# Two chunks of keys in one product: the intra-chunk levels of the recurrences in a two-layer hybrid decoder step

## The chip, the cores and the metric

The kernel runs on one core of one Trainium2 chip (trn2). The metric is the time of one execution in microseconds (us), taken on the device. The kernel before ran three times, at 1866.79 to 1868.54 us with a median of 1867.7 us. A fourth execution was recorded by the hardware profiler; its rows are the ones shown here.

The engines go by short names: PE is TensorE's matmul, PEld its load of the stationary operand, DVE is VectorE, ACT is ScalarE, POOL is GpSimd, SP is SyncE, which only starts DMAs.

## The reference, cut to what matters

The program is two decoder layers over 512 prompt positions and 64 positions of eight short sequences (eight positions each). In each layer a token mixer has three groups of heads. Six heads are windowed attention. The other ten, four HGRN2 heads with 64 keys' features and six GLA heads with 32, are gated linear recurrences, which the reference computes in chunks of 64 positions:

```python
def step(S, blk):
    qc, kc, vc, gc = blk
    b = jnp.cumsum(gc, axis=1)
    o_inter = jnp.einsum('bthk,bhkv->bthv', qc * jnp.exp(b), S)
    diff = b[:, :, None] - b[:, None, :]
    decay = jnp.exp(jnp.where(causal, diff, -jnp.inf))
    A = jnp.einsum('bthk,bshk,btshk->bths', qc, kc, decay)
    o_intra = jnp.einsum('bths,bshv->bthv', A, vc)
```

The change is about `A`, the 64 x 64 matrix of each head and chunk. Its decay depends on the pair of positions and on the feature, so it is no plain product of queries and keys. After the mixer come the output projection, an MLP of width 4096 with squared ReLU and a gated per-layer embedding.

## The kernel before, in words

All tensors are feature-major: features on the 128 partitions, the 576 positions along the row. Weights come in units of 128 x 1024 numbers. Each is split by ACT and DVE into a leading and a remaining part, and each product with weights is three `fp32r` products (lines 738 to 742 in the mixer, 1684 to 1686 in the MLP) that move 288 positions past a stationary 128 x 128 block.

`A` is built by levels. `LEVELS` is 0, 1, 2, 4, 8, 16, 32. Level 0 is the diagonal. At a level of size h each chunk is cut into blocks of 2h positions; every pair (key in the earlier half of a block, query in the later half) belongs to this level, and there the decay falls apart into a factor for the key and one for the query, both measured from the block's middle. DVE takes the differences (`diff`, lines 1443 and 1444), ACT exponentiates them (`decays`, line 1200), and DVE multiplies the earlier halves with the keys and the later halves with the queries (`scale`, lines 1450 and 1452). So `LV[l % 2]`, the tile that the level's products read, holds keys in the earlier half of each block and queries in the later.

The products of a level run by `GROUPS`: four groups of two heads and two of one. For each head, PE multiplies keys and queries of each of the eight chunks, 64 keys stationary and 64 queries moving (line 887), and writes chunk c to the upper or lower 64 partitions of a PSUM bank by c's parity. The tile is used as keys and as queries at once, so only a part of each 64 x 64 result means anything. The groups take turns on two banks; a group waits until DVE has emptied the one before the last (`lv_ev`). DVE's `pick` copies the entries that the level's mask names into `AT` with one predicated copy a group (line 1470, 512 or 256 numbers in each of 128 partitions). In the levels that fit in eight positions (sizes 0 to 4, `SMALL`) line 898 adds one 64 x 64 product a head for the short sequences, and line 1478 its copy.

The order around the levels is written out by hand. In levels 0 to 5 PE does 18 products of one projection between groups 1 and 2 and the other 30 after group 5 (`project`). In levels 4 to 6 it also does the partners of the rotary embedding (line 861) ahead of groups 2 and 4, which ACT copies (line 1234) and DVE's `rotate` uses (lines 1457 to 1460). PE enters a level when DVE has scaled it (`lv_ready`). After level 6 PE multiplies `AT` by the values (lines 916 and 924), and the attention begins. SP starts the first keys' loads after the last `lv_ready`, the others after the last projection.

All products of the levels are full fp32: each shows in the trace as two records of LDWEIGHTS and MATMUL.

Of the kernel before, what the change touches and what calls it, by code (L numbers as in the profile page):

```python
# [16 lines left out]
P = 128  # L17
# [211 lines left out]
def build(nc, x_t, consts, params, w_first, p_t, s0_in, w_units, ck, cv,  # L229
          y_out, kp_out, kn_out, vp_out, vn_out, ck_out, cv_out, sp_out, ss_out):  # L230
    with ExitStack() as ctx:
# [183 lines left out]
        for layer in range(DEPTH):  # L415
# [233 lines left out]
            def _(pe):  # L649
# [216 lines left out]
                for l in range(len(LEVELS)):  # L866
# [7 lines left out]
                    for g, heads in enumerate(GROUPS):  # L874
# [6 lines left out]
                            pe.wait_ge(*at(lv_ev, gi - 1))  # L881
                        for i, h in enumerate(heads):
                            r, row, n = HEAD_AT[h]
                            for c in range(NC):
                                o = 64 * (c % 2)
                                col = (4 * i + c // 2) * CH
                                mm = nc.tensor.matmul(b_[o:o + 64, col:col + CH],  # L887
                                                      kq[0][row:row + n, r, c * CH:(c + 1) * CH],
                                                      kq[1][row:row + n, r, c * CH:(c + 1) * CH], start=True, stop=True)
                        mm.then_inc(*up(lv_mm, 1))  # L890
                        gi += 1
                        if l in SMALL:
# [441 lines left out]
            def _(dve):  # L1334
# [129 lines left out]
                def pick(l):  # L1464
                    nonlocal gi, si
                    mask = con[:, C_MASK + CH * l:C_MASK + CH * (l + 1)].bitcast(U32).rearrange("p (a t) -> p a t", a=1)
                    for g, heads in enumerate(GROUPS):
                        n, s = len(heads), FIRST_SLOT[g]
                        dve.wait_ge(*at(lv_mm, gi + 1))
                        nc.vector.copy_predicated(  # L1470
                            AT[:, s:s + n].rearrange("p s c t -> p (s c) t"), mask.to_broadcast([P, 4 * n, CH]),
                            bank[4 + gi % 2][:, 0:4 * n * CH].rearrange("p (a t) -> p a t", t=CH)).then_inc(*up(lv_ev, 1))
                        gi += 1
                        if l >= 4 and g == 1:
                            rotate(2 * l - 8)
                        if l in SMALL:
                            dve.wait_ge(*at(ls_mm, si + 1))
                            nc.vector.copy_predicated(
                                ATS[0:NEW, s:s + n], mask[0:NEW].to_broadcast([NEW, n, CH]),
                                bank[6 + si % 2][0:NEW, 0:n * CH].rearrange("p (a t) -> p a t", t=CH)).then_inc(*up(ls_ev, 1))  # L1480
                            si += 1
# [829 lines left out]
```

## Time and profile before

| | us |
|---|---|
| median of three runs | 1867.7 |
| the profiled execution's own time | 1867.47 |
| its span, first to last instruction | 1865.7 |
| PE busy / PEld busy in the span | 1769.5 / 1646.6 |
| DVE busy / ACT busy | 858.2 / 653.0 |
| line 887, PE busy, both layers | 75.4 |
| line 1470, DVE busy, both layers | 52.6 |

The last number is the sum of two groups, 40.5 us for the copies of 512 numbers and 12.1 us for those of 256. "Busy" is time covered by at least one record. Matmuls overlap in their pipeline and the ends of their records are modelled, so the distance from one record's start to the next says more about PE than a record's duration does; where equal instructions are merged into one row, x32 with 1.15 us means that 32 of them covered 1.15 us. Levels 0 to 6 run from 186.9 to 278.1 us in the first layer and from 1107.7 to 1206.4 us in the second.

### The profile page before, as it was taken

To read this page: it belongs to the slowest core of one execution; us is meant where nothing else is said; L and a number is where in the kernel's file an instruction comes from. 1 tells how busy PE (TensorE), PEld (TensorE's weight loads), DVE (VectorE), ACT (ScalarE), POOL (GpSimd) and SP (SyncE) were. 2 spreads that over 40 slices of the span, in tenths; PEclk is the share of its full clock that TensorE was granted. 3 is DMA by queue.
4 is the path that set the end of the run, shared out by engine and by line. 5 is a ranking of instruction groups with operands and counts; after the bars stand their busy time and mean duration, and the time that the engine had idled before them with its cause. 6 is when DMAs were issued, how large, how long until landed. Compare 5 with 4: busy or idle time off the path is not lost.

```text
span 1865.7 us, 35758 instructions
## 1 busy us (share of the span) xinstructions
PE 1769.5 (95%) x16070; PEld 1646.6 (88%) x16070; DVE 858.2 (46%) x1311; ACT 653.0 (35%) x963; POOL 71.1 (4%) x90
## 2 busy tenths in 40 slices
PE   6999998899999999999889999987999999999998
PEld 5988985588999999998888888845989999999988
DVE  5514885336423333346544157844354133333365
ACT  5422425544423222233344232245344231222233
POOL 0012110000000000000000130100000000000000
PEclk9999998899999999999989998988999999999999
DMA  7521428851836625442353132388419366355311
GB/s 265 179 68 60 160 82 338 306 179 69 310 125 216 217 101 205 158 137 68 111 206 110 58 132 77 123 336 297 155 64 317 123 214 217 110 193 181 123 58 63
DMA packets 60649, 303.67 MB, mean 163 GB/s; under 512 B 7120, under 2 KB 8784, under 8 KB 58832
## 3 DMA queue, kind: packets, MB, share of 16 engines
q1 hardware_dynamic: 53072, 200.91, 30.1%
q0 software_dynamic: 7424, 100.47, 15.4%
q8 instruction: 127, 2.08, 0.5%
q14 instruction: 26, 0.21, 0.0%
HBM read 290.74 MB, written 111.08 MB: 215 GB/s over the span
## 4 chain that ended last, share of the span: by engine, by line
PE 88%; DVE 7%; ACT 3%; issue 2%; DMA 1%; SPq 0%; DVEq 0%; ACTq 0%
PE pair L1684 15%; PE pair L1686 14%; PE pair L1685 14%; PE pair L887 3%; PE pair L738 3%; PE pair L740 2%; PE pair L742 2%; PE pair L720 2%; PE pair L670 2%; PE pair L721 2%; PE pair L722 2%; PE pair L671 2%; PE pair L672 2%; PE pair L1764 2%; PE pair L996 1%
## 5 line engine op out<-in xcount | busy, mean ns | idle before, releaser
L1684 PE MATMUL pair<-x_hi_part,w_hi_part 128*128 128x288 f32 x1088 | 322.2, 296 | 2.0 <-DVE tmp L2063 2.0
L1685 PE MATMUL pair<-x_lo_part,w_hi_part 128*128 128x288 f32 x1088 | 321.0, 295 | 0.0
L1686 PE MATMUL pair<-x_hi_part,w_lo_part 128*128 128x288 f32 x1088 | 319.9, 294 | 0.0
L2000 DVE TENSOR_TENSOR w_lo_part<-raw,w_hi_part 128x1024 fp32r<-128x1024 f32 x154 | 188.7, 1225 | 234.8 <-ACT w_hi_part L1851 234.8
L1684 PE MATMUL pair<-u_hi_part,w_hi_part 128*128 128x288 f32 x928 | 274.7, 296 | 0.0
L1685 PE MATMUL pair<-u_lo_part,w_hi_part 128*128 128x288 f32 x928 | 273.8, 295 | 0.0
L1686 PE MATMUL pair<-u_hi_part,w_lo_part 128*128 128x288 f32 x928 | 272.8, 294 | 0.0
L1851 ACT ACTIVATE w_hi_part<-raw 128x1024 fp32r<-128x1024 f32 x154 | 161.8, 1051 | 209.6 <-PE pair L1686 208.3
L1684 PEld LDWEIGHTS pair<-x_hi_part,w_hi_part 128*128 128x128 f32 x1088 | 203.9, 187 | 2.5 <-DVE tmp L2063 2.5
L1686 PEld LDWEIGHTS pair<-x_hi_part,w_lo_part 128*128 128x128 f32 x1088 | 204.9, 188 | 0.0
L1685 PEld LDWEIGHTS pair<-x_lo_part,w_hi_part 128*128 128x128 f32 x1088 | 204.3, 188 | 0.0
L1686 PEld LDWEIGHTS pair<-u_hi_part,w_lo_part 128*128 128x128 f32 x928 | 174.8, 188 | 0.0
L1685 PEld LDWEIGHTS pair<-u_lo_part,w_hi_part 128*128 128x128 f32 x928 | 174.2, 188 | 0.0
L1684 PEld LDWEIGHTS pair<-u_hi_part,w_hi_part 128*128 128x128 f32 x928 | 173.9, 187 | 0.0
L1340 DVE TENSOR_TENSOR win_part<-raw,win_part 128x1024 fp32r<-128x1024 f32 x54 | 65.9, 1224 | 175.0 <-ACT win_part L1103 174.9
L1915 ACT ACTIVATE tmp<-tmp 128x576 f32<-128x576 f32 x64 | 44.0, 687 | 255.6 <-DVE tmp L2063 255.6
L738 PE MATMUL pair<-xn_hi_part,win_part 128*128 128x288 f32 x352 | 114.6, 326 | 0.0
L2063 DVE SCALAR_TENSOR_TENSOR tmp<-pair,tmp 128x576 f32<-128x576 f32 x64 | 48.5, 757 | 135.6 <-PE pair L1686 122.1
L740 PE MATMUL pair<-xn_lo_part,win_part 128*128 128x288 f32 x352 | 109.8, 312 | 0.0
L742 PE MATMUL pair<-xn_hi_part,win_part 128*128 128x288 f32 x352 | 109.6, 311 | 0.0
L2072 DVE TENSOR_TENSOR y<-y,pair 128x576 f32<-128x576 f32 x42 | 31.7, 755 | 157.6 <-PE pair L1686 157.6
L670 PE MATMUL pair<-xn_hi_part,win_part 128*128 128x288 f32 x256 | 79.0, 308 | 10.2 <-DVE xn_lo_part L1340 9.9
(282 smaller groups left out, 3552.3 us busy)
## 6 DMA issues: line engine op xcount, KB each, us to landing
raw<-w_units SPq DMA_DIRECT2D x210, 512.0 KB, 3.6
ck_out<-ck POOLq DMA_DIRECT2D x16, 3060.0 KB, 14.0
arena<-cv SPq DMA_DIRECT2D x24, 640.0 KB, 7.8
tail<-cv SPq DMA_DIRECT2D x24, 640.0 KB, 7.9
arena<-ck SPq DMA_DIRECT2D x18, 640.0 KB, 10.1
more<-ck SPq DMA_DIRECT2D x18, 640.0 KB, 12.9
h<-ck SPq DMA_DIRECT2D x12, 640.0 KB, 12.7
y_out<-h SPq DMA_DIRECT2D x16, 288.0 KB, 2.1
```

The source lines that it names most:

```text
L670: nc.tensor.matmul(out, wh[:, cols], XH[:, k, t], start=k == 0, stop=False)
L738: mm = nc.tensor.matmul(out, wh[:, cols], XH[:, k, t], start=k == 0, stop=False)
L740: mm = nc.tensor.matmul(out, wh[:, cols], XL[:, k, t], start=False, stop=False)
L742: mm = nc.tensor.matmul(out, wl[:, cols], XH[:, k, t], start=False, stop=k == KT - 1)
L887: mm = nc.tensor.matmul(b_[o:o + 64, col:col + CH], kq[0][row:row + n, r, c * CH:(c + 1) * CH], kq[1][row:row + n, r, c * CH:(c + 1) * CH] ...
L1340: return tt_(dst, src, hi.bitcast(F32), ALU.subtract).then_inc(*up(done, 1))
L1684: nc.tensor.matmul(out, wh[:, cols], xh[:, k, t], start=n == 0, stop=False)
L1685: nc.tensor.matmul(out, wh[:, cols], xl[:, k, t], start=False, stop=False)
L1686: mm = nc.tensor.matmul(out, wl[:, cols], xh[:, k, t], start=False, stop=n == KT - 1)
L1851: return A(dst, src, ACT.Copy).then_inc(*up(done, 1))
L2000: return tt_(dst, src, hi.bitcast(F32), ALU.subtract).then_inc(*up(done, 1))
L2063: stt(two(t), home(f"up{g}")[:, :, 0:HALF], 0.0, two(RS), ALU.max, ALU.mult).then_inc(*up(lin_ev, 1))
```

## The change

In levels 1 to 6 a product takes the 128 positions of two neighbouring chunks as the stationary operand, and moves 64 queries: of both chunks only the later halves of the blocks, picked by a strided view. The result covers 128 partitions (the keys of both chunks) by 64 columns (32 late queries of the first chunk, then 32 of the second). What meets across the two chunks is not used. Four products a head and level stand where eight did, 40 a level for the ten heads. Level 0 keeps its form.

DVE's copy is split by the parity of the chunk: one takes partitions 0 to 63 with the columns of the even chunks, the other partitions 64 to 127 with those of the odd ones. Each handles half as many numbers in a partition, in 64 partitions, and writes to and masks by strided views. Two instructions a group stand where one did; the second signals.

```diff
-                            for c in range(NC):
-                                o = 64 * (c % 2)
-                                col = (4 * i + c // 2) * CH
-                                mm = nc.tensor.matmul(b_[o:o + 64, col:col + CH],
-                                                      kq[0][row:row + n, r, c * CH:(c + 1) * CH],
-                                                      kq[1][row:row + n, r, c * CH:(c + 1) * CH], start=True, stop=True)
+                            if l == 0:
...
+                            else:
+
+                                for c2 in range(TT):
+                                    t, col = slice(2 * c2 * CH, 2 * (c2 + 1) * CH), (4 * i + c2) * CH
+                                    late = kq[1][row:row + n, r, t].rearrange("p (b a e) -> p b a e", a=2, e=LEVELS[l])[:, :, 1]
+                                    mm = nc.tensor.matmul(b_[:, col:col + CH].rearrange("p (b e) -> p b e", e=LEVELS[l]),
+                                                          kq[0][row:row + n, r, t], late, start=True, stop=True)
...
+                            e = LEVELS[l]
+                            late = mask.rearrange("p z (b a e) -> p z b a e", a=2, e=e)[:, :, :, 1]
+                            for par_ in range(2):
+                                rows = slice(64 * par_, 64 * par_ + 64)
+                                dst = AT[rows, s:s + n].rearrange("p s c (b a e) -> p (s c) b a e", a=2, e=e)[:, :, :, 1]
+                                src = bank[4 + gi % 2][rows, 0:4 * n * CH].rearrange("p (x z b e) -> p x z b e", z=2, e=e, b=CH // 2 // e)
+                                ins = nc.vector.copy_predicated(dst, late[rows].to_broadcast([64, 4 * n, CH // 2 // e, e]), src[:, :, par_])
+                            ins.then_inc(*up(lv_ev, 1))
```

On PE, the first two groups of level 1 in the first layer, between two projections. The shape is that of the output, partitions by columns; line 896 is the new product and line 906 the old line 898.

```order
 L742 MATMUL pair<-xn_hi_part_104,win_part_106 128x288
-L887 MATMUL pair<-arena 64x64 x16
-L898 MATMUL pair<-arena 64x64 x2
-L887 MATMUL pair<-arena 64x64 x16
-L898 MATMUL pair<-arena 64x64 x2
+L896 MATMUL pair<-arena 128x64 x8
+L906 MATMUL pair<-arena 64x64 x2
+L896 MATMUL pair<-arena 128x64 x8
+L906 MATMUL pair<-arena 64x64 x2
 L738 MATMUL pair<-xn_hi_part_104,win_part_107 128x288
```

Nothing changes place: the groups, the products for the short sequences and the projections follow each other as before, with half as many products of 128 output partitions in a group. Every neighbour of a line-906 product inside these groups now has another output shape.

On DVE, the end of the picks of level 1 in the first layer, first of the kernel before.

```order
L1470 COPY_PREDICATED tail<-con,pair 128x512
L1478 COPY_PREDICATED tail<-con,pair 64x128
L1470 COPY_PREDICATED tail<-con,pair 128x256
L1478 COPY_PREDICATED tail<-con,pair 64x64
L1450 TENSOR_TENSOR arena<-arena 128x576x2
```

The same place in the changed kernel, where 1490 is the line of the split copy and 1458 that of the first multiplication.

```order
L1490 COPY_PREDICATED tail<-con,pair 64x256 x2
L1497 COPY_PREDICATED tail<-con,pair 64x128
L1490 COPY_PREDICATED tail<-con,pair 64x128 x2
L1497 COPY_PREDICATED tail<-con,pair 64x64
L1458 TENSOR_TENSOR arena<-arena 128x576x2
```

Two copies of half the length stand where one stood, and the rest keeps its order.

## Rows read from the trace of the kernel before

**Rows 1.** The page: busy time of each engine, and the chain that ended last.
```profile
PE 1769.5 (95%) x16070; PEld 1646.6 (88%) x16070; DVE 858.2 (46%) x1311; ACT 653.0 (35%) x963; POOL 71.1 (4%) x90
...
PE 88%; DVE 7%; ACT 3%; issue 2%; DMA 1%; SPq 0%; DVEq 0%; ACTq 0%
```

**Rows 2.** Stretches of both layers' levels: PE, PEld, DVE, ACT, POOL busy, clock, DMA.
```profile
186.90:278.10 91.20, 88.03 (x1515) 81.50 (x1514) 75.73 (x109) 29.93 (x28) 12.20 (x15) 0.96 0.32 115
...
1110.00:1207.00 97.00, 92.27 (x1460) 85.59 (x1463) 75.70 (x110) 27.63 (x26) 12.24 (x15) 0.89 0.30 109
```

**Rows 3.** PE, line 887's groups by form: count, busy us, mean ns, idle before.
```profile
L887 PE MATMUL pair<-arena 32*64 32x64 f32 x1344 | 46.2, 223 | 3.1 <-DVE tail L1470 3.1
...
L887 PE MATMUL pair<-arena 64*64 64x64 f32 x896 | 29.2, 224 | 3.7 <-DVE arena L1452 3.7
```

**Rows 4.** Timeline of level 6, first layer, PE alone: start us, us covered, line, idle before.
```profile
269.54 1.91 PE L887 MATMUL pair<-arena 64*64 64x64 f32 x64
271.38 1.24 PE L861 MATMUL pair<-tail,con 128*128 128x288 f32 x4
...
276.26 1.29 PE L887 MATMUL pair<-arena 32*64 32x64 f32 x32 [0.63 <-DVE tail L1470]
```

**Rows 5.** Timeline, level 0 begins: start us, us covered, engine, line, count, idle before.
```profile
186.67 0.29 PE L742 MATMUL pair<-xn_hi_part,win_part 128*128 128x288 f32 x1
186.89 1.15 PE L887 MATMUL pair<-arena 64*64 64x64 f32 x32
...
188.86 0.39 PE L898 MATMUL pair<-arena 64*64 64x64 f32 x4
...
189.19 0.40 PE L738 MATMUL pair<-xn_hi_part,win_part 128*128 128x288 f32 x1
```

**Rows 6.** Timeline in narrow windows: line 861, first and third of three records.
```profile
271.73 0.41 PE L861 MATMUL pair<-tail,con 128*128 128x288 f32 x1
...
272.21 0.41 PE L861 MATMUL pair<-tail,con 128*128 128x288 f32 x1
```

**Rows 7.** Durations of one line's records (min/median/max ns): 32, 64, 128 stationary columns.
```profile
L988 PEld LDWEIGHTS pair<-tail,arena x96: 106/110/110, 285.8 to 1275.3; 128*32 128x32 f32 x96
...
L887 PEld LDWEIGHTS pair<-arena x32: 129/135/135, 186.9 to 187.8; 64*64 64x64 f32 x32
L887 PE MATMUL pair<-arena x30: 218/218/267, 186.9 to 187.8; 64*64 64x64 f32 x30
...
L861 PEld LDWEIGHTS pair<-tail,con x4: 186/190/190, 271.4 to 272.0; 128*128 128x128 f32 x4
L861 PE MATMUL pair<-tail,con x4: 406/406/510, 271.4 to 272.2; 128*128 128x288 f32 x4
```

**Rows 8.** Timeline at 186.89 us, narrow windows: loads of line 887 come in pairs.
```profile
186.89 0.14 PEld L887 LDWEIGHTS pair<-arena 64*64 64x64 f32 x2 [0.17 <-issue]
...
186.89 0.19 PEld L887 LDWEIGHTS pair<-arena 64*64 64x64 f32 x4 [0.17 <-issue]
```

**Rows 9.** Timeline: 32 records that move 8 columns past 64 stationary, and what follows.
```profile
165.70 1.10 PE L795 MATMUL pair<-tail 64*64 64x8 f32 x32
166.63 0.89 PEld L802 LDWEIGHTS pair<-tail 64*64 64x64 f32 x27
```

**Rows 10.** Timeline, narrow windows: attention scores, two row halves, 128 stationary columns each.
```profile
312.72 0.19 PEld L948 LDWEIGHTS pair<-tail 64*128 64x128 f32 x2 [0.17 <-issue]
...
312.83 0.19 PEld L948 LDWEIGHTS pair<-tail 64*128 64x128 f32 x2
```

**Rows 11.** Timeline near 132 us: first and third of three records of a projection.
```profile
132.10 0.29 PE L738 MATMUL pair<-xn_hi_part,win_part 128*128 128x288 f32 x1
...
132.36 0.30 PE L742 MATMUL pair<-xn_hi_part,win_part 128*128 128x288 f32 x1
```

**Rows 12.** DVE, groups by form: count, busy us, mean ns, idle before.
```profile
L1470 DVE COPY_PREDICATED tail<-con,pair 128x512 f32<-128x512 uint32 x56 | 40.5, 740 | 14.7 <-PE pair L887 14.1
...
L1470 DVE COPY_PREDICATED tail<-con,pair 128x256 f32<-128x256 uint32 x28 | 12.1, 441 | 5.4 <-PE pair L887 5.2
L1478 DVE COPY_PREDICATED tail<-con,pair 64x128 f32<-64x128 uint32 x32 | 9.0, 282 | 0.0
```

More of the change, by code:

```diff
@@ L883, in _ @@
                             r, row, n = HEAD_AT[h]
-                            for c in range(NC):
-                                o = 64 * (c % 2)
-                                col = (4 * i + c // 2) * CH
-                                mm = nc.tensor.matmul(b_[o:o + 64, col:col + CH],
-                                                      kq[0][row:row + n, r, c * CH:(c + 1) * CH],
-                                                      kq[1][row:row + n, r, c * CH:(c + 1) * CH], start=True, stop=True)
+                            if l == 0:
+                                for c in range(NC):
+                                    o = 64 * (c % 2)
+                                    col = (4 * i + c // 2) * CH
+                                    mm = nc.tensor.matmul(b_[o:o + 64, col:col + CH],
+                                                          kq[0][row:row + n, r, c * CH:(c + 1) * CH],
+                                                          kq[1][row:row + n, r, c * CH:(c + 1) * CH], start=True, stop=True)
+                            else:
[4 more added lines that the diff above has]
+                                                          kq[0][row:row + n, r, t], late, start=True, stop=True)
                         mm.then_inc(*up(lv_mm, 1))
@@ L1469, in pick @@
                         dve.wait_ge(*at(lv_mm, gi + 1))
-                        nc.vector.copy_predicated(
-                            AT[:, s:s + n].rearrange("p s c t -> p (s c) t"), mask.to_broadcast([P, 4 * n, CH]),
-                            bank[4 + gi % 2][:, 0:4 * n * CH].rearrange("p (a t) -> p a t", t=CH)).then_inc(*up(lv_ev, 1))
+                        if l == 0:
+                            nc.vector.copy_predicated(
+                                AT[:, s:s + n].rearrange("p s c t -> p (s c) t"), mask.to_broadcast([P, 4 * n, CH]),
+                                bank[4 + gi % 2][:, 0:4 * n * CH].rearrange("p (a t) -> p a t", t=CH)).then_inc(*up(lv_ev, 1))
+                        else:
+                            e = LEVELS[l]
[6 more added lines that the diff above has]
+                            ins.then_inc(*up(lv_ev, 1))
                         gi += 1
```

## The prediction

> **What bounds the kernel now.** I read the page first. The reader is to see PE busy for 95% of the span, and a chain that ended last of which 88% is PE [rows 1]. What lengthens PE in a stretch without idle time lengthens the kernel. Then I cut out the levels: in the first layer PE is busy for 88.0 of 91.2 us, in the second for 92.3 of 97.0, while DVE is busy for 75.7 in each [rows 2]. So here too PE sets the end, and DVE has 15 us or more of room a layer. Then the waits of line 887: 3.1 us in both layers for DVE's copies and 3.7 us for its scaling [rows 3]. A gain on DVE could give back at most these 6.8 us. The question is what a product of the new form costs PE.
>
> **What a product costs PE.** Each full fp32 product is two records, each with its own load of the stationary operand. I take distances between starts. In level 6 two groups, 64 records, run from 269.54 to the start of line 861 at 271.38 [rows 4]: 1.84 us, 29 ns each, and 27 when 0.09 are taken off for the change of shape behind them (below). In level 0, 32 records cover 1.15 us; less the 0.22 of the last one that is 0.93 us over 31 distances, 30 ns [rows 5], with a slower first one in it. I take 28 ns: a level of 160 records is 4.5 us, with bounds of 4.4 (27 ns) and 4.9 (30.6 ns, 0.98 us a group).
>
> Which part binds, stream or load? Line 861 moves 288 columns past a 128-column operand with (272.21 - 271.73) / 2 = 0.24 us between starts [rows 6], 0.83 ns a column, so 64 columns stream in 53 ns. The loads: medians are 110, 135 and 190 ns for 32, 64 and 128 stationary columns [rows 7], about 0.83 ns more for each column, over a constant of some 83. The constant is latency, the rest is occupation: 27, 53 and 107 ns. A second row says the same. The first record of a run has nothing to hide its load behind, and is longer than its successors by 510 - 406 = 104 ns with 128 columns and by 267 - 218 = 49 ns with 64 [rows 7].
>
> How, then, can line 887 start a record every 28 ns? Its loads come in pairs: two are done within the first 0.14 us, four within 0.19 [rows 8], one pair every 50 to 60 ns. Neighbouring chunks go to the lower and the upper 64 columns of the array, and each half works for itself: 53 to 60 ns a record in a half, two halves at once. That this is the load and not the stream is shown by line 795, which moves only 8 columns and still needs 166.63 - 165.70 = 0.93 us for 32 records, 29 ns each, 58 in a half [rows 9].
>
> The new product takes all 128 columns. There is no second half to run beside it, its heads share their rows within a group, and one load lasts 107 ns and covers the 53 ns of the stream. Line 948 is the nearest row with 64 x 128 operands: its two first loads go at once to two different row halves, and each half's next one comes 0.11 us later [rows 10]. So the distance is 107 ns: half as many records, each nearly four times as far apart, 80 x 0.107 = 8.6 us a level instead of 4.5, +4.1. For six levels in two layers: **+49.2 us**. Bounds: from 4.9 us before, 8.56 - 4.90 = 3.66, or +43.9; and at the 131 ns (132.36 - 132.10 over two [rows 11]) of the projections' chain, which has a load of the same width behind a stream of 288 columns, 10.5 - 4.4 = 6.1, or +73. That chain is fp32r, with a longer stream, so the loads' own rows are nearer and I stay with them.
>
> The Trainium skill, "TensorE: Matmul & The Clock Gate", section "LDWEIGHTS (loading the stationary operand)", gives columns divided by 1.2 as the load's nanoseconds, 107 for 128 and 53 for 64. By this rule the sum is the same; what speaks against the change is only its consequence, that the column count and not the number of instructions is paid. The same page's tiling part says that a load overlaps running matmuls only when the row group differs. By that rule the sum would be another: see the third rival.
>
> **Changes of shape.** Before, lines 887 and 898 follow each other in one shape. Now the products for the short sequences (64 output partitions) stand between products of 128. Such a change is seen at 186.67: the first load of line 887 comes 0.22 us after line 742's start, where the distance in the chain is 0.13 [rows 11], and then waits 0.05 for its load, 0.14 in all. On the way back line 738 comes 0.16 us after the last start of line 898 (188.86 + 0.17 = 189.03), where 0.06 were usual: 0.10 [rows 5]. Mean 0.12. In levels 1 to 3 there are 3 such changes in the first block and 7 in the second, 10 a level, 60 in both layers: **+7.2 us**. Bounds 0 and 0.20 each, 0 to 12 us. The Trainium skill, "TensorEngine Tiling (Array Packing)", section "Key Properties", says that changing the tiling mode drains TensorE. The trace agrees, with 0.22 against 0.13.
>
> **DVE.** The copy of 512 takes 740 ns and that of 256 takes 441, 1.17 ns a number over some 140; 128 numbers then take 290, and the row of a 128-number copy says 282 [rows 12]. A double group costs 2 x 441 instead of 740, +0.14; a single one 2 x 282 instead of 441, +0.12. Per level 4 x 0.14 + 2 x 0.12 = +0.8, per layer +4.9. No row shows copies with such strides. Between no penalty and half the rate (1.17 ns more a number: 256 x 1.17 = 0.30 for each of eight copies and 0.15 for each of four, +3.0 a level), I take none, since the operands' strides are small. Either way it lies beside PE: DVE's 75.7 us become 81 or, at worst, 99, while the stretch becomes 118. Only the very last copies of level 6 are on the path, at +0.1 us. **0 us**. If PE were not slower, this cover would be gone: the fourth rival.
>
> **Waits given back.** Line 887's 3.1 us of waiting for copies [rows 3] come from groups that PE finishes faster than DVE empties the bank (0.9 us and 0.45 against 0.74 and 0.44). Now a group takes 1.7 or 0.86 us and DVE is in time; 0.63 of it is in level 6 [rows 4], where DVE rotates in between. Level 0's part stays. **-2.5 us**. The 3.7 us for the scaling [rows 3] stay: the products of level 0 ahead of them aren't changed. What is late next is nothing; PE runs through. **Low clock:** of the new time a few per cent fall where the granted clock is 1.2 GHz (mean 0.96 and 0.89 [rows 2]) and count double: 5 to 10% of it in the second layer would be +2; most such places are at the entry of level 1, so **+1 us**. SP and POOL issue what they did, later with everything else.
>
> Sum: 49.2 + 7.2 + 0 - 2.5 + 1 = +54.9 us. The profiled execution took 1867.47 us, 1.8 outside its span and 0.2 below the median, so 1867.5 + 54.9 = 1922.4, and **1922 us**.
>
> **The rivals.**
> 1. Loads wait in one queue, at 28 ns for 64 columns and 56 for 128. The even distance of lines 887 and 795 allows this reading. Then 80 x 0.056 = 4.5, no change on PE; shape changes +7.2 and waits -2.5 remain: 1872. Against it: two loads within 0.14 us [rows 8], and the first record's 104 ns.
> 2. Faster. The full-width load uses the paths of both halves, 53 ns, so that only the stream of 53 ns binds: 80 x 0.053 = 4.24, -0.26 a level, -3.1 in twelve; the waits go too, -2.5, and if shape changes within the same rows cost nothing, 1862. It decides as soon as the distance between records falls under 56 ns. For it: half the loads and half the instructions. Against it the same 104 ns: line 861 is a full-width load, and its first record shows what it takes.
> 3. Load and stream of one tile don't overlap (the page's rule above, as a mechanism here): 107 + 53 + 5 = 165 ns, 80 x 0.165 = 13.2, +8.7 a level, +104 in all, and +5.7 as above: about 1977. Against it line 861's 0.24 us, which is the stream alone, with a load of 104 ns hidden in the same rows [rows 6].
> 4. DVE takes the end, if 1 or 2 holds for PE and strided copies run at half rate: DVE needs 75.7 + 4.9 + 18 = 99 us a layer in a stretch of 91 to 97, +5 to +8 a layer and more where it is late already: about 1885.
> 5. The clock. PE streams less in a microsecond now. If the granted clock falls to 1.2 GHz for a sixth of the work of the levels, 2 x 118 / 6 = 39 us of it take twice as long: 1922 + 39, about 1960. For it: the second layer's levels already run at a mean of 0.89 [rows 2]. Against it: the first layer's, with the same products, run at 0.96, and no row shows the clock falling inside an unbroken run of them.
>
> **How the numbers follow.** A measurement of this kernel tells 0.2%, 3.7 us, from no change. The forecast gets 0.78, rival 1 0.07, rival 2 0.06, rival 3 0.03, rival 4 0.01, rival 5 0.05. Rival 1's 1872 lies at the edge; I give 0.04 of it to no change. So faster 0.06, same 0.04, slower 0.90. The forecast's own range is 1867.5 + 43.9 - 2.5 = 1909 to, with both upper bounds at once, 1867.5 + 73 + 12 + 1 - 2.5 = 1951; I cut the top at 1945, since the two rarely meet. I lower the low end to 1900, for waits given back that I don't see, and leave the rivals out, some 0.2 in all.
>
> **What would show it.** The new line has 80 records a level, some 107 ns apart, a double group in 1.7 us, its loads 186 to 190 ns long. Line 906 in levels 1 to 3 has gaps of 0.1 to 0.2 us around it. Levels 0 to 6 take about 118 us in the first layer instead of 91. PE no longer waits for the copies in levels 1 to 5. The split copies take 0.44 and 0.28 us. Distances of 55 to 61 ns would refute the step on the load, copies of 0.7 us the one on DVE, and low clock within the levels would make rival 5 real.

## The result and the profile after

The changed kernel takes 1962.1 us (median of 4 runs, 1955.1 to 1975.0) against 1868.1 us before on the same chip: a ratio of 1.053, 95% interval 1.050 to 1.056, or +94 us. The forecast was 1922 us with a range of 1900 to 1945. The direction was right and the size was not: the time lies 17 us above the range. The profiled execution is the longest of the four, 1975.0 us, so it shows some 13 us more than the median. Two single slow runs of the experiments below, 3441 us in e4 and 3396 us in e6, were repeated by no other run of their kernels, and the medians leave them out.

These are rows of its page: busy time of each engine, the granted clock of PE in 40 slices, and the chain that ended last. They answer to [rows 1].

```profile
PE 1876.8 (95%) x15110; PEld 1746.9 (89%) x15110; DVE 886.7 (45%) x1383; ACT 653.1 (33%) x963; POOL 71.7 (4%) x90
...
PEclk9999677889999999999989996778899999999999
...
PE 90%; DVE 5%; ACT 3%; issue 1%; DMA 1%; SPq 0%; DVEq 0%; ACTq 0%
```

PE has 960 instructions less and 107 us more of busy time, and bounds the kernel as before. A digit stands for 49.3 us. The digits 6, 7, 7 lie in the two places where the levels are; the two 8s stand behind the levels, where the kernel before has 8s too. So the span was cut into stretches: from the first product of level 0 to the first product that uses the levels' result, and what lies between and behind. Columns: from:to, length, busy time of PE, PEld, DVE, ACT and POOL with counts, granted clock, DMA share, GB/s. First the kernel after:

```profile
185.00:337.00 152.00, 148.46 (x1035) 138.13 (x1035) 90.04 (x146) 30.10 (x28) 13.19 (x17) 0.74 0.25 88
337.00:1164.60 827.60, 789.32 (x6523) 735.02 (x6523) 350.63 (x544) 293.25 (x449) 22.50 (x27) 0.97 0.47 164
1164.60:1316.50 151.90, 148.41 (x1033) 138.08 (x1032) 89.99 (x145) 30.10 (x28) 13.20 (x17) 0.74 0.25 89
1316.50:1973.20 656.70, 622.99 (x5115) 586.32 (x5115) 280.85 (x458) 231.37 (x367) 6.68 (x12) 0.97 0.50 174
```

The same stretches of before (the first layer's is in [rows 2]; the second layer's was shown there with other ends):

```profile
278.10:1107.60 829.50, 791.82 (x6523) 737.03 (x6523) 350.59 (x544) 293.43 (x449) 22.50 (x27) 0.97 0.47 167
1107.60:1206.40 98.80, 94.11 (x1513) 87.35 (x1512) 75.81 (x110) 29.91 (x28) 12.89 (x17) 0.90 0.31 111
1206.40:1865.70 659.30, 626.25 (x5115) 589.65 (x5115) 280.82 (x458) 231.44 (x367) 6.68 (x12) 0.96 0.50 177
```

Everything is in the levels: 152.0 + 151.9 against 91.2 + 98.8 us, +113.9; the rest of the span is 6 us shorter. The granted clock of the levels fell from 0.96 and 0.90 to 0.74. A mean of 0.74 means that 52% of the time passes at 1.2 GHz, the other level being 2.4. Length times mean clock estimates what a stretch would take at full clock (waits are scaled too, so it is rough): 87.6 and 88.9 us before, 112.5 in both layers after. So about +49 us is more work for PE, and about +65 us in this execution is clock. The split is good to a few us only: level 0 of the first layer is 15.4 us long before (clock 0.89) and 15.5 after (1.00), and counts as 1.8 us of added work; and a projection's products go from 0.13 to 0.24 us apart in the low clock, which is less than twice, so that work done there is counted too low.

**The work.** Two rows of the new line's records in level 2 (ns: least, median, most; then first and last start):

```profile
L896 PEld LDWEIGHTS pair<-arena x16: 182/188/189, 228.0 to 229.7; 64*128 64x128 f32 x16
L896 PE MATMUL pair<-arena x16: 268/270/323, 228.0 to 229.8; 64*128 64x64 f32 x16
```

And the timeline of PE around them (start, us covered, line, form, count):

```profile
227.81 0.29 PE L742 MATMUL pair<-xn_hi_part,win_part 128*128 128x288 f32 x1
228.03 2.00 PE L896 MATMUL pair<-arena 64*128 64x64 f32 x16
229.96 0.44 PE L906 MATMUL pair<-arena 64*64 64x64 f32 x4
230.33 2.00 PE L896 MATMUL pair<-arena 64*128 64x64 f32 x16
232.26 0.44 PE L906 MATMUL pair<-arena 64*64 64x64 f32 x4
232.63 0.45 PE L738 MATMUL pair<-xn_hi_part,win_part 128*128 128x288 f32 x1
```

Sixteen records cover 2.00 us; less the first one's 0.32 that is 1.68 over 15 distances, 112 ns. The loads last 188 ns, as one of 128 columns does [rows 7]. In level 4 nothing stands between the first two groups, whose heads lie in rows 0 to 63 and in rows 64 to 127:

```profile
281.85 3.39 PE L896 MATMUL pair<-arena 64*128 64x64 f32 x32
```

Records 112 ns apart would cover 31 x 0.112 + 0.32 = 3.79 us. The difference is where the groups meet: around 283.4 us the records start 54 to 58 ns apart, the end of one group beside the start of the next in the other rows.

**The clock.** The first layer in windows of 5 us, the kernel after (columns as above):

```profile
205.00:210.00 5.00, 5.00 (x24) 4.76 (x24) 2.49 (x5) 0.10 (x1) 0.00 (x0) 0.50 0.10 39
...
220.00:225.00 5.00, 5.00 (x22) 4.76 (x23) 3.74 (x7) 0.00 (x0) 0.00 (x0) 0.50 0.00 0
225.00:230.00 5.00, 5.00 (x37) 4.77 (x36) 3.38 (x4) 1.86 (x3) 0.00 (x0) 0.90 0.00 0
...
245.00:250.00 5.00, 5.00 (x22) 4.76 (x22) 3.72 (x8) 0.00 (x0) 0.00 (x0) 0.50 0.00 0
...
285.00:290.00 5.00, 5.00 (x37) 4.56 (x35) 3.62 (x7) 1.00 (x2) 0.00 (x0) 1.00 0.02 3
...
295.00:300.00 5.00, 5.00 (x21) 4.93 (x21) 4.71 (x7) 0.00 (x0) 0.00 (x0) 0.50 0.00 0
```

PE is busy for all of each window, and whole windows pass at 0.50. The fall comes again and again inside unbroken work, which the prediction held unlikely because no row of before shows it.

### The profile page after: what moved, and what is told of

It reads as the page before. It is cut to its first block, busy times and chain, and to the rows that moved or that the text cites. A ratio compares the mean times of both kernels' runs of the same rounds, so it can differ in the third digit from the quotient of the medians.

```text
span 1973.2 us, 33910 instructions
## 1 busy us (share of the span) xinstructions
PE 1876.8 (95%) x15110; PEld 1746.9 (89%) x15110; DVE 886.7 (45%) x1383; ACT 653.1 (33%) x963; POOL 71.7 (4%) x90
## 4 chain that ended last, share of the span: by engine, by line
PE 90%; DVE 5%; ACT 3%; issue 1%; DMA 1%; SPq 0%; DVEq 0%; ACTq 0%
PE pair L1703 14%; PE pair L1705 14%; PE pair L1704 14%; PE pair L896 7%; PE pair L738 3%; PE pair L740 3%; PE pair L742 3%; PE pair L720 2%; PE pair L721 2%; PE pair L722 2%; PE pair L670 2%; PE pair L672 2%; PE pair L671 2%; PE pair L1783 2%; PE pair L1004 1%
## 5 line engine op out<-in xcount | busy, mean ns | idle before, releaser
L896 PEld LDWEIGHTS pair<-arena 32*128 32x128 f32 (+1 forms) x960 | 132.9, 230 | 16.1 <-DVE arena L1460 5.7
L896 PE MATMUL pair<-arena 32*128 32x64 f32 (+1 forms) x960 | 141.9, 320 | 5.3 <-DVE arena L1460 5.3
L738 PE MATMUL pair<-xn_hi_part,win_part 128*128 128x288 f32 x352 | 123.7, 352 | 0.0
L740 PE MATMUL pair<-xn_lo_part,win_part 128*128 128x288 f32 x352 | 118.1, 335 | 0.0
L742 PE MATMUL pair<-xn_hi_part,win_part 128*128 128x288 f32 x352 | 117.9, 335 | 0.0
L1490 DVE COPY_PREDICATED tail<-con,pair 64x256 f32<-64x256 uint32 (+1 forms) x144 | 67.0, 465 | 94.9 <-PE pair L896 93.8
```

The lines of the kernel that those rows point to most:

```text
L738: mm = nc.tensor.matmul(out, wh[:, cols], XH[:, k, t], start=k == 0, stop=False)
L740: mm = nc.tensor.matmul(out, wh[:, cols], XL[:, k, t], start=False, stop=False)
L742: mm = nc.tensor.matmul(out, wl[:, cols], XH[:, k, t], start=False, stop=k == KT - 1)
L896: mm = nc.tensor.matmul(b_[:, col:col + CH].rearrange("p (b e) -> p b e", e=LEVELS[l]), kq[0][row:row + n, r, t], late, start=True, stop=True)
L1490: ins = nc.vector.copy_predicated(dst, late[rows].to_broadcast([64, 4 * n, CH // 2 // e, e]), src[:, :, par_])
```

## The experiments

Ten kernels ran, each timed against the kernel before on the same chip, but not all on one chip. Rows of theirs are from the profiled execution.

### What a product costs: short loads (e1, e2, e6)

The first asks whether the load's width or the shorter stream is paid. It keeps the late queries and the split copies, but gives each product one chunk's keys, 64 columns, in alternating halves of the array:

```diff
-for c2 in range(TT):
-    t, col = slice(2 * c2 * CH, 2 * (c2 + 1) * CH), (4 * i + c2) * CH
+for c in range(NC):
+    o = 64 * (c % 2)
+    col = (4 * i + c // 2) * CH + 32 * (c % 2)
+    t = slice(c * CH, (c + 1) * CH)
...
-    mm = nc.tensor.matmul(b_[:, col:col + CH].rearrange("p (b e) -> p b e", e=LEVELS[l]),
+    mm = nc.tensor.matmul(b_[o:o + 64, col:col + CH // 2].rearrange("p (b e) -> p b e", e=LEVELS[l]),
                           kq[0][row:row + n, r, t], late, start=True, stop=True)
```

> Levels 1 to 6 with the old 64-key stationary blocks (80 products a level), each moving only the 32 late queries of its own chunk, and the changed kernel's split copies. The shape of every product stays 64 output partitions. Theory A (the price is the load: 107 ns for 128 columns, and the shape changes): loads go in pairs again, 27 ns a record, so the levels take the time of before, 91 us in the first layer; 1868 us plus at most 5 for the copies. Theory B (clock follows the work of the array, which here is half of before per unit of time, as in the changed kernel): the distances are as in A while the clock is full, but the granted clock of the stretch falls from 0.96 towards 0.72, and the projections in it slow down: some 1890 us. Theory C (the clock falls because of idle gaps and exposed loads at the shape changes, not because of the array's work): clock stays at 0.96 and time at 1868 to 1873.

Measured: 1889.1 us, ratio 1.012 (1.008 to 1.016). The second keeps the products of before and only splits the copies:

```diff
-                            if l == 0:
+                            if True:
                                 for c in range(NC):
...
-src = bank[4 + gi % 2][rows, 0:4 * n * CH].rearrange("p (x z b e) -> p x z b e", z=2, e=e, b=CH // 2 // e)
-ins = nc.vector.copy_predicated(dst, late[rows].to_broadcast([64, 4 * n, CH // 2 // e, e]), src[:, :, par_])
+src = bank[4 + gi % 2][rows, 0:4 * n * CH].rearrange("p (x b a e) -> p x b a e", a=2, e=e, b=CH // 2 // e)
+ins = nc.vector.copy_predicated(dst, late[rows].to_broadcast([64, 4 * n, CH // 2 // e, e]), src[:, :, :, 1])
```

> The products of before, with the split and strided copies of the changed kernel (two of 64 partitions by 256 or 128 numbers a group). All theories give PE the same work as before. If the copies are hidden, 1868 us. The trace of the changed kernel has copies of up to 0.74 us for 256 numbers where 0.44 was expected, so that DVE gains up to 3.8 us a level over before in the small ones: then PE waits at the entry of the levels, and the time is 1868 + 10 to 25 us.

Measured: 1888.1 us, 1.011 (1.007 to 1.015). The third has the 40 products a level of the change with 64 moving columns, but loads only the first chunk's 64 key columns; the results for the second chunk's keys are left out:

```diff
-mm = nc.tensor.matmul(b_[:, col:col + CH].rearrange("p (b e) -> p b e", e=LEVELS[l]),
-                      kq[0][row:row + n, r, t], late, start=True, stop=True)
+mm = nc.tensor.matmul(b_[0:CH, col:col + CH].rearrange("p (b e) -> p b e", e=LEVELS[l]),
+                      kq[0][row:row + n, r, 2 * c2 * CH:(2 * c2 + 1) * CH], late, start=True, stop=True)
```

> The changed kernel with 40 products a level and 64 moving columns, but only the keys of the first of the two chunks stationary, 64 columns in the lower half of the array (the results for the second chunk's keys are left out; the copies run over stale numbers). If a load costs by its columns, and nothing runs beside it in one half, records are 53 to 58 ns apart, 80 of them in 4.5 us: the levels at full clock take the 91 to 92 us of the experiment with the copies alone, and the shape changes are gone: 1888 us. If the number of records or the form of the moving operand were the cost, the distance would stay 107 ns and the time 1940 to 1960 us. Theory B on the clock: a stream of 53 ns in 53 to 58, in half of the array only; the clock should stay at the 0.89 of the copies-alone kernel if the share of time with a stream counts, and fall if the number of working cells counts.

Measured: 1883.7 us (three runs), 1.010 (1.007 to 1.014). The first layer's levels in the kernel with short loads and half streams:

```profile
187.50:293.40 105.90, 97.19 (x1517) 90.31 (x1516) 89.15 (x146) 29.90 (x28) 13.20 (x17) 0.87 0.31 111
```

The same in the one with the copies alone:

```profile
186.80:289.70 102.90, 95.95 (x1515) 88.60 (x1514) 89.04 (x145) 29.90 (x28) 12.49 (x15) 0.89 0.29 106
```

And with half-width loads:

```profile
188.40:292.40 104.00, 97.86 (x1035) 90.76 (x1034) 88.48 (x146) 29.90 (x28) 13.15 (x17) 0.87 0.32 112
```

All three are alike, 103 to 106 us, against 152 after. The number of products (80 or 40) and the moving columns (64 or 32) don't tell; only the 128 columns of the load do, with the 128 output partitions that go with them. The last kernel has the records, the streams and the copies of the one after, with half the load's width, and is 78 us faster. Some 6 to 7 of them are for the changes of shape, which go too, since all outputs have 64 partitions, and a large part is clock, 0.87 against 0.74. Without both, in level 4 at full clock, it shows the width alone:

```profile
253.01:266.58 13.57, 13.57 (x137) 12.35 (x136) 11.20 (x21) 4.58 (x5) 0.00 (x0) 1.00 0.01 1
```

The kernel before, with twice as many records, takes 13.47 us for this level, and the products with wide loads 17.22 (both rows stand in the next section). So the step on the load stands.

All three are also 1.0 to 1.2% slower than before, some 20 us; that is little, but none of the three intervals includes 1. What they have in common is the split copies. Groups by form of the kernel with the copies alone (busy, mean ns, idle before and who ended it); they answer to [rows 3, 12]:

```profile
L888 PE MATMUL pair<-arena 32*64 32x64 f32 x1344 | 51.3, 231 | 10.3 <-DVE tail L1490 9.7 <-DVE tail L1479 0.4
...
L1490 DVE COPY_PREDICATED tail<-con,pair 64x256 f32<-64x256 uint32 x96 | 50.9, 531 | 3.1 <-PE pair L888 1.7
```

PE waits 9.7 us for copies instead of 3.1, and DVE for PE 1.7 instead of 14.1: in places DVE has become the bound. In the first layer's level 1 DVE is busy for 16.25 of 16.55 us in this kernel:

```profile
202.19:218.74 16.55, 14.87 (x228) 13.87 (x228) 16.25 (x25) 2.69 (x2) 0.00 (x0) 0.90 0.22 73
```

The same level in the one before:

```profile
202.31:215.04 12.73, 12.54 (x228) 11.95 (x229) 11.68 (x18) 2.69 (x2) 0.00 (x0) 1.00 0.25 84
```

At full clock the levels are 91.6 us a layer against 88.2 before (mean of the layers), +7 us in the two together. In the profiled execution, the fastest of the four, the levels are 16 us longer in all, so the other 9 are clock: 0.89 in both layers, although PE has the same products as before. The kernel of e5 below differs from the one of e1 in little but the copies (one instead of two a group), and there the 20 us are gone.

### What lowers the clock (e3, e4, e7, e8, e9, e10)

The clock's share could come from the shorter streams behind long loads (B in the expectations), from the small gaps at the changes of shape (C), or from the length of the unbroken stretches of such products (E). First: the loads of the change, but 128 columns moved past nearly every one of them. The late queries go through twice; products run in reverse order, so that the first of the two results lands in columns that the next product writes over.

```diff
-    mm = nc.tensor.matmul(b_[:, col:col + CH].rearrange("p (b e) -> p b e", e=LEVELS[l]), ..., late, ...)
+    twice = 2 if j > 0 else 1
+    late = late.to_broadcast([n, twice, CH // e, e])
+    mm = nc.tensor.matmul(b_[:, (j + 1 - twice) * CH:(j + 1) * CH].rearrange("p (x b e) -> p x b e", x=twice, e=e), ..., late, ...)
```

> The changed kernel with each product of the levels 1 to 6 moving its 64 late queries twice (128 columns; the first copy lands in the columns that the next product overwrites). Loads as in the changed kernel, 107 ns, and a stream of 128 x 0.83 = 107 ns beside it. Theory A (loads and shape changes alone) gives the distance 107 to 115 ns and the time of the changed kernel, 1955 to 1970 us, or a little more. Theory B (the clock follows the array's work): the clock of the stretch comes back from 0.72 to above 0.9, and the time falls although each product does more, to about 1925 us, which is what the forecast gave without a fall of the clock. Theory C (gaps and exposed loads lower the clock): clock and time stay as in the changed kernel.

Measured: 1948.0 us, 1.042 (1.039 to 1.046), 14 us below the kernel after (19 by the two ratios to before) although it streams nearly twice as much. Its first layer's levels, then level 4 alone:

```profile
185.10:321.40 136.30, 132.78 (x1035) 123.25 (x1034) 90.15 (x146) 29.99 (x28) 13.28 (x17) 0.84 0.27 96
...
272.83:290.05 17.22, 17.22 (x137) 15.99 (x136) 11.24 (x20) 4.70 (x5) 0.00 (x0) 1.00 0.00 1
```

Level 4 in the kernel after:

```profile
281.85:301.95 20.10, 20.10 (x138) 18.82 (x137) 13.98 (x23) 4.70 (x5) 0.00 (x0) 0.83 0.00 1
```

In the one before:

```profile
242.04:255.51 13.47, 13.47 (x218) 12.25 (x217) 11.39 (x15) 4.59 (x5) 0.00 (x0) 1.00 0.01 2
```

And in the next experiment, e4:

```profile
244.99:265.11 20.12, 20.12 (x137) 18.84 (x136) 13.71 (x23) 4.70 (x5) 0.00 (x0) 0.83 0.00 1
```

That level has no change of shape that the kernel before lacks and, in the kernels with 13.47 and 17.22 us, full clock and no idle time: the wide loads alone cost 17.22 - 13.47 = 3.75 us a level. Length times clock gives 16.7 us for the same level of the kernel after, half a microsecond less, which shows how rough that reckoning is.

Second: the new form in levels 4 to 6 only, where no product of another shape stands between.

```diff
-                            if l == 0:
+                            if l < 4:
```

> The new products and copies in levels 4 to 6 only, where no product for the short sequences stands between them; levels 0 to 3 as before. Theory A without shape changes: 3 levels x 2 layers x 4.1 us = +25, 1893 us. Theory B adds the slow clock in these levels, half of the changed kernel's surplus or less: about 1868 + 40 = 1908 us, with the granted clock of levels 4 to 6 well under 0.9. If the clock falls only because of the gaps in levels 1 to 3, it stays at 1.0 here and the time is 1890 to 1895.

Measured: 1894.5 us (three runs, 1893.5 to 1909.7), 1.017 (1.011 to 1.022). Its level 4 is the last row above: 20.12 us at 0.83, as in the kernel after. The clock falls with no change of shape added, so C as the whole cause is out. The time is close to the 1893 us that theory A gave for the loads alone, but by luck. The first layer's levels:

```profile
186.80:297.30 110.50, 108.05 (x1273) 101.64 (x1272) 79.26 (x126) 30.14 (x28) 12.51 (x15) 0.86 0.32 118
```

At full clock they would take some 95 us against 88 before: about 7 us a layer more work, not 12, and the rest is clock.

Third and fourth: 64-column loads with each product done twice, with half streams (e1 doubled) and with full ones (e2 doubled), so that the stretches are as long as after:

```diff
+for _ in range(2):            # the second: range(1 if l == 0 else 2)
     mm = nc.tensor.matmul(...)
```

> The first experiment (64 keys stationary, 32 late queries moving) with each product done twice: 160 products a level, 27 ns a record, 8.7 us a level, as long as the changed kernel's products, without wide loads and without shape changes, and each stream half as long as its load. Theory B (long stretches in which the array streams half of the time lower the clock): clock about 0.75 to 0.8 in the stretch, levels 4 and 5 at 0.76 to 0.83 as in the changed kernel, 1945 to 1960 us. Theory C (gaps and shape changes): clock 0.87 or better, +4.3 x 12 = +52 on 1889 with at most 10 less for waits hidden: 1930 to 1940 us. It is read beside the next one.

> The same doubling with 64 moving columns (the products of before, each twice, with the split copies): loads, distances, shapes and number of records as in the half-stream kernel, but each stream as long as its load. Theory B: the clock stays where the array streams all the time, levels 4 and 5 at 1.00, so this kernel is faster than the half-stream one although it streams twice as much, by 15 us or more: 1920 to 1935 us. Theory C: the same clock and time as the half-stream kernel.

Measured: 1948.8 us, 1.045 (1.041 to 1.048), and 1952.6 us, 1.047 (1.044 to 1.050). First layer's levels with half streams:

```profile
188.60:320.70 132.10, 130.08 (x2475) 123.06 (x2474) 89.31 (x146) 30.00 (x28) 13.15 (x17) 0.84 0.29 105
```

And with full ones:

```profile
186.50:322.70 136.20, 132.65 (x2476) 125.05 (x2475) 89.82 (x146) 30.01 (x28) 13.20 (x17) 0.83 0.29 102
```

Twice the streamed columns change nothing: 0.84 and 0.83 (0.82 in both in the second layer). B as the whole cause is out too. What the three kernels with long levels (e3 and these two) share is that PE works longer than before on fp32 products with 32 or 64 rows of the array; each has a mean of 0.82 to 0.84, and only the kernel after, with 64 columns behind a 128-column load, is at 0.74. That this is the cause is an inference from them, not shown by itself, and it can't be all: in e1, e2 and e6 the clock fell to 0.87 to 0.89 with no more of these products to do.

Fifth and sixth: the projections, which stand in two blocks a level, are spread over all groups in levels 1 to 5, so that no stretch of small products is longer than one group. Once on the kernel after, once on the version with one copy (below):

```diff
-                        if g == 2 and l < len(LEVELS) - 1:
+                        if g >= 1 and 1 <= l < len(LEVELS) - 1:
+                            project(5 + l, *(0, 6, 12, 16, 20, 22)[g - 1:g + 1])
+                        if g == 2 and l == 0:
                             project(5 + l, 0, 18)
...
-                        project(5 + l, 18)
+                        project(5 + l, 18 if l == 0 else (0, 6, 12, 16, 20, 22)[-1])
```

> The changed kernel, with the projection of levels 1 to 5 spread between all groups (6, 6, 4, 4 and 2 of its 48 products after groups 0 to 4, the other 26 at the end) instead of 18 and 30. All work is the same; the longest unbroken run of the small fp32 products falls from some 6 us to 2. It adds three pairs of shape changes a level, about 0.25 us each: +0.75 x 10 = +7.5 us at full clock. The doubled products have shown that the clock falls where such products run long, with half or full streams alike. Theory E (it is the length of an unbroken block of small products that lowers the clock): mean clock of the stretch from 0.74 to 0.85 or more, 1962 + 8 - 35 = 1935 us. Theory F (the share of small products over a longer time counts, not how they are spread): clock as it was, 1970 us.

> The kernel with late queries moving and one copy (products and loads as before the change, 1864 us), with the same spreading of the projections. Its levels 2 and 3 had a clock of 0.78 and 0.88. Theory E: clock of the stretch from 0.93 to 0.98 or more, 4 us a layer back, against 7.5 us of shape changes: 1862 to 1866 us. Theory F: clock as it was, 1871 us.

Measured: 1991.6 us, 1.068 (1.065 to 1.072), 30 us more than after; and 1899.0 us, 1.018 (1.015 to 1.021), 35 us more than without the spreading. Both lie over 20 us above what either theory gave. First layer's levels of the kernel after, spread:

```profile
185.40:340.40 155.00, 154.13 (x1033) 140.37 (x1032) 89.72 (x146) 30.13 (x28) 13.13 (x17) 0.74 0.24 84
```

Of the version with one copy, spread:

```profile
186.80:291.20 104.40, 102.36 (x1513) 91.88 (x1512) 69.70 (x109) 30.02 (x28) 12.04 (x15) 0.89 0.27 96
```

The clock didn't come back: 0.74 as after, and 0.89 where the undivided version has 0.93 (in the second layer 0.86 against 0.94). E as the whole cause is out; since the spreading also adds changes of shape, a small part of it could be hidden. Dividing costs twice, in changes of shape (length times clock rises by 2 to 5 us a layer in the first, by some 7 in the second) and in clock. That the changes themselves lower the clock, each with a load that nothing hides, fits the last pair but was not tried alone.

### One copy (e5)

Late queries with 64-column loads, both chunks' results in the same columns of the bank, so that one copy on 128 partitions takes a group: half the numbers of before, and half the instructions of the change.

```diff
-    t, col = slice(2 * c2 * CH, 2 * (c2 + 1) * CH), (4 * i + c2) * CH
+    o = 64 * (c % 2)
+    col = (4 * i + c // 2) * (CH // 2)
+    t = slice(c * CH, (c + 1) * CH)
...
-for par_ in range(2):
...
+src = bank[4 + gi % 2][:, 0:2 * n * CH].rearrange("p (x b e) -> p x b e", e=e, b=CH // 2 // e)
+ins = nc.vector.copy_predicated(dst, late.to_broadcast([P, 4 * n, CH // 2 // e, e]), src)
```

> The one part of the change that costs PE nothing, kept alone: 64-key stationary blocks for each chunk as before (80 products a level, loads in pairs), only the 32 late queries moving, and the results of both parities in the same 32 columns, so that one copy of 128 partitions by 256 or 128 numbers serves a group. PE as in the kernel before. DVE: levels 3 to 6 pay 0.44 and 0.28 us for what were 0.74 and 0.44, levels 1 and 2, whose runs of 1 and 2 numbers were seen at 0.74 for 256, pay what they did. If waits for the copies are the only thing left to give back: 1866 minus 2 to 4 us, 1862 to 1864. If the half stream lowers the clock by itself, as theory B has it, 1866 or more. If the long copies of levels 1 and 2 don't come from the short runs but from the 64 partitions, they too become faster, and the time is 1860.

Measured: 1864.1 us (12 runs, 1854.8 to 1869.5) against 1866.8 us (17 runs): 0.999 (0.997 to 1.001), not told apart from before. Both layers' levels and the group of the copies:

```profile
186.40:278.20 91.80, 89.40 (x1513) 83.38 (x1512) 69.23 (x110) 29.90 (x28) 12.68 (x17) 0.93 0.33 116
1110.80:1201.40 90.60, 87.88 (x1513) 81.95 (x1512) 69.33 (x109) 29.91 (x28) 12.06 (x15) 0.94 0.32 113
...
L1490 DVE COPY_PREDICATED tail<-con,pair 128x256 f32<-128x256 uint32 x48 | 24.7, 532 | 11.8 <-PE pair L898 11.5
```

DVE saves 6.5 us a layer and at full clock the levels take 85.3 us instead of 88.2, but PE stays the bound, and of those 6 us in two layers the median shows 2.7, within its uncertainty. The idea of the change is sound as far as DVE goes; there is little to be had there.

## Why the prediction was wrong

**What bounds the kernel:** right. PE sets the end before and after, and all of the difference is in the levels.

**The load, 107 ns instead of 28, +49.2 us:** right. The distance is 112 ns in level 2, the loads last 188 ns, and the undisturbed level 4 gives +3.75 us, where 4.1 was forecast; neighbouring groups in different rows overlap there, which the forecast left out. Twelve levels at 3.75 are 45 us, inside its bounds of 43.9 and 73. The half-width experiment shows that the width is what is paid. Rivals 1 and 2 (56 or 53 ns) are refuted, and rival 3 (165 ns) too.

**Changes of shape, +7.2 us:** right in the place where it was read. From L742 to the new line the starts are 228.03 - 227.81 = 0.22 us apart, where 0.13 are usual; from the last new record, at 228.03 + 2.00 - 0.27 = 229.76, to L906 it is 0.20, where 0.11 is. Levels 1 to 3 take 4.7 to 5.0 us more than before at full clock (first layer 12.7, 12.5 and 12.8 us, now 17.4, 17.5 and 17.5, all by length times clock), for level 1 from this row:

```profile
200.46:228.03 27.57, 27.57 (x148) 25.82 (x148) 17.72 (x25) 2.12 (x1) 0.00 (x0) 0.63 0.22 72
```

That is 1.0 to 1.2 more than level 4's 3.75 for 10 changes, and up to 1.8 more than the 3.2 that level 4 of the kernel after gives by the same reckoning; forecast was 1.2. It includes the overlap of neighbouring groups, which level 4 has and these levels lack.

**The copies, 0 us:** the time stands in this kernel, since PE became slower, but the working was off. Runs of one or two numbers (levels 1 and 2) take nearly twice as long as longer ones. The timeline of DVE after, two copies of 256 each in level 1 and in level 3:

```profile
204.00 1.46 DVE L1490 COPY_PREDICATED tail<-con,pair 64x256 f32<-64x256 uint32 x2
...
257.03 0.86 DVE L1490 COPY_PREDICATED tail<-con,pair 64x256 f32<-64x256 uint32 x2
```

That is the upper bound of the prediction in two levels of six and its value in four; DVE came to 90 us a layer, between 81 and 99. Without the cover these copies cost some 20 us, by rival 4's mechanism. It was tied to rivals 1 and 2 and so didn't count here.

**Waits, -2.5 us:** right in kind, too large in sum. The new line no longer waits for copies; only line 924 behind it sits idle, for 0.70 us in the first layer, until the last copy of level 6 is done. But the 5.3 us for the scaling, taken to stay at 3.7, are the entry to level 1, 2.64 in each layer: DVE sets when level 0 ends, and PE, whose clock was 1.00 there instead of 0.89 in the first layer, came to that point earlier. By the rows of the stretches PE is idle for 7.9 us in the levels before and for 7.0 after, so 0.8 came back. PE's groups by form, after:

```profile
L896 PE MATMUL pair<-arena 32*128 32x64 f32 x576 | 91.0, 334 | 0.0
...
L896 PE MATMUL pair<-arena 64*128 64x64 f32 x384 | 50.9, 298 | 5.3 <-DVE arena L1460 5.3
```

**Low clock, +1 us: this is the step that failed.** The sum without it was 53.9 us; measured at full clock it is 2 x 112.5 - 87.6 - 88.9 = 48.5, good to a few us. The rest of the stretches' +113.9, about 65 us in the profiled execution and some 50 by the median, is the clock. The prediction took the share of low clock from before (a few per cent) and carried it over to work of another kind. Rival 5 named this mechanism and came out at 1960 us, 2 us from the measured time, but got a chance of 0.05. That its number came so close is luck: it let a sixth of the levels' work run at 1.2 GHz, while a mean of 0.74 means over a third, and it stood on a sum that was some 5 us too high. Its reason against, that no row shows the clock falling in an unbroken run of the levels' products, was an absence of evidence: the kernel before has no such run of this length. And its trace did hold windows in the first layer's levels in which PE is busy throughout and the clock is down:

```profile
195.00:200.00 5.00, 5.00 (x40) 4.93 (x35) 4.84 (x5) 0.92 (x1) 4.65 (x2) 0.66 1.18 430
...
225.00:230.00 5.00, 5.00 (x51) 4.83 (x52) 4.22 (x4) 0.61 (x2) 0.00 (x0) 0.84 0.00 0
```

Most of what runs there is projection, close behind the levels' products, but they show that full busy time didn't hold the clock. The second layer's 0.89 in [rows 2], with the same products as the first layer's 0.96, showed that the same work can run at either; that should have widened the range to 1960 at least. Rival 5's own reason, that PE streams less in a microsecond, holds only in part: it fits 0.84 with full streams and 0.74 with half ones under 128-column loads, but not the equal 0.84 and 0.83 under 64-column loads.

What stays open is the rule. The runs show what the clock doesn't follow alone (PE's busy share, the changes of shape, the streamed columns, the length of the stretches) and that it was lower wherever PE had more of the small fp32 products to do: from about 0.93 before to 0.83 with levels of 132 to 139 us, at two different stream lengths. It also fell, to 0.87 to 0.89, where only the copies became slower. No experiment varied the rows of the products or their type by itself.

## What to carry to other kernels

Before merging small products into wider ones, price each by the columns of its stationary operand: two 64-column products in the two halves of the array are loaded at once, one of 128 columns takes the array alone, and here cost nearly four times as much a record. If a change keeps PE on small products for longer, take the clock as a term of the sum with its own range, from zero to as much as the added work, since a clock that is seen at two values for the same products can't be counted on. And an edit that is free because another engine is slow is to be priced for the case that it isn't: the split copies were hidden here, and alone cost 20 us.

## What was not expected of the hardware

- The granted clock falls to 0.50 within windows in which PE is busy for 5.00 of 5.00 us, and moving 128 columns instead of 64 past the same loads raised the levels' mean from 0.74 to 0.84 and made the kernel 14 us faster.
- A predicated copy of 256 numbers a partition takes 0.74 us where its operands' runs are one or two fp32 numbers long, and 0.44 with runs of four or more; it takes the same on 64 partitions and on 128 (means over all levels 528 and 532 ns).
- The projections, too, run slower in the low clock: near 280 us in the kernel after they start every 0.24 us instead of 0.13 (279.54, 279.78, 280.02), so that a fall is paid by all the work that runs while it lasts.
